# Six modulation weights summed on VectorE instead of multiplied on TensorE, and the first projection reordered

## What is computed

```python
mod_x = (jax.nn.silu(c) @ w_mod[i] + b_mod[i])[:, None, :]
mod_c = jax.nn.silu(c_ctx) @ w_mod[i] + b_mod[i]
sh1x, sc1x, g1x, sh2x, sc2x, g2x = jnp.split(mod_x, 6, axis=-1)
hx = modulate(rmsnorm(x, norm1_g[i]), sh1x, sc1x)
hc = modulate(rmsnorm(ctx, norm1_g[i]), sh1c, sc1c)
c_dq, c_dk, c_dv, c_gq, c_gk, c_gv = _mixer_heads(hc @ w_in[i])
x_dq, x_dk, x_dv, x_gq, x_gk, x_gv = _mixer_heads(hx @ w_in[i])
...
out_x = _mix_queries(...)          # differential + grouped attention, then w_out
x = x + g1x * out_x
hx2 = modulate(rmsnorm(x, norm2_g[i]), sh2x, sc2x)
x = x + g2x * peer(hx2, ...)       # 16 experts of 8 heads gathered per token
```

## Time and profile before

| | us |
|---|---|
| median of 3 runs | 1664.56 |
| lowest and highest run | 1661.77, 1664.97 |
| the profiled execution, its own time | 1663.03 |
| its span in the profile | 1661.2 |
| TensorE busy | 1407.2 |
| VectorE busy | 1086.2 |
| ScalarE busy | 617.1 |

### The profile page before, as it was taken

One profiled execution on the slowest core, in us unless ns is written; L12 is line 12 of the kernel. 1 busy time (PEld: TensorE's weight loads), 2 busy tenths in 40 slices (PEclk: granted clock), 3 DMA queues, 4 the chain that ended last, 5 costly groups with the idle time before them and its releaser, 6 DMA issues.

```text
span 1661.2 us, 20184 instructions
## 1 busy us (share of the span) xinstructions
PE 1407.2 (85%) x6400; PEld 968.6 (58%) x6400; DVE 1086.2 (65%) x2240; ACT 617.1 (37%) x1213; POOL 278.9 (17%) x263
## 2 busy tenths in 40 slices
PE   7897989578787878787877848978999889889998
PEld 2784666334343434343433317668999776689986
DVE  3667864666767676667677536647887366378863
ACT  4344642122222222222222114445665344456652
POOL 0000000444444444444444300000000000000000
PEclk9999989789898989899989978989999999899999
DMA  9423430799999999999999943133444431335440
GB/s 400 176 102 112 192 123 26 295 421 421 421 422 423 422 422 422 422 422 422 422 421 422 422 175 111 67 113 142 175 181 178 179 127 51 125 130 188 168 178 26
DMA packets 49267, 418.04 MB, mean 252 GB/s; under 512 B 5408, under 2 KB 5536, under 8 KB 6560
## 3 DMA queue, kind: packets, MB, share of 16 engines
q0 software_dynamic: 36864, 268.45, 38.9%
q1 hardware_dynamic: 12320, 148.51, 23.3%
HBM read 415.89 MB, written 1.05 MB: 251 GB/s over the span
## 4 chain that ended last, share of the span: by engine, by line
PE 57%; DMA 18%; DVE 8%; issue 8%; POOL 5%; ACT 3%; POOLq 0%; DVEq 0%; ACTq 0%; SPq 0%
DMA arena<-in_uv,ids 18%; PE ps L938 9%; PE ps L1134 5%; PE ps L1133 5%; PE ps L1135 5%; POOL arena L666 4%; PE ps L1009 4%; PE ps L1011 4%; PE ps L1010 4%; PE ps L918 2%; PE ps L1001 2%; PE ps L1059 2%; PE ps L788 2%; PE ps L790 2%; PE ps L789 2%
## 5 line engine op out<-in xcount | busy, mean ns | idle before, releaser
L938 PE MATMUL ps<-ring,arena 128*128 128x512 f32 x512 | 255.9, 662 | 105.4 <-ACT arena L1305 105.4
L536 DVE TENSOR_TENSOR arena_r<-ring,arena_r 128x1024 fp32r<-128x1024 f32 x168 | 204.7, 1224 | 89.2 <-ACT arena_r L530 89.1
L938 PE MATMUL ps<-arena 128*128 128x512 f32 x512 | 228.9, 606 | 31.3 <-ACT arena L1305 31.0
L938 PEld LDWEIGHTS ps<-ring,arena 128*128 128x128 f32 x512 | 107.8, 214 | 249.1 <-issue 133.0
L1739 DVE CUSTOM_DVE_ANT_0 arena<-arena 128x1024 f32<-128x1024 f32 x128 | 155.3, 1225 | 129.9 <-DMA arena<-in_uv,ids 129.7
L1305 ACT ACTIVATE arena<-cst,wts 128x128 f32<-128x128 f32 x256 | 89.5, 394 | 388.6 <-DVE wts L1731 272.5
L666 POOL DMA_INDIRECT ring<-in_uv,ids x128 | 134.8, 1053 | 549.0 <-issue 329.0
L530 ACT ACTIVATE arena_r<-ring 128x1024 fp32r<-128x1024 f32 x168 | 175.9, 1053 | 84.6 <-PE ps L1011 84.6
L1133 PE MATMUL ps<-hH,arena_r 128*128 128x256 f32 x704 | 199.4, 283 | 0.0
L1134 PE MATMUL ps<-arena_r 128*128 128x256 f32 x704 | 199.2, 283 | 0.0
L1135 PE MATMUL ps<-hH,arena_r 128*128 128x256 f32 x704 | 199.2, 283 | 0.0
(11 more groups left out here) (279 smaller groups left out, 2076.7 us busy)
## 6 DMA issues: line engine op xcount, KB each, us to landing
ring<-in_lw SPq DMA_DIRECT2D x42, 2048.0 KB, 8.4
ring<-in_b1w SPq DMA_DIRECT2D x18, 2048.0 KB, 7.7
wqb<-in_wq SPq DMA_DIRECT2D x8, 1024.0 KB
ring<-in_lw SPq DMA_DIRECT2D x6, 1024.0 KB, 5.0
ring<-in_uv,ids POOLq DMA_INDIRECT x128, 17.0
arena<-in_uv,ids POOLq DMA_INDIRECT x128, 18.7
cst<-in_const SPq DMA_DIRECT2D x1, 1736.0 KB, 20.0
skb<-in_ctx SPq DMA_DIRECT2D x1, 1024.0 KB, 14.2
```

The source lines that it names most:

```text
L536: nc.vector.tensor_tensor(wL[p % PIECES], piece_raw(p), wH[p % PIECES].bitcast(F32), ALU.subtract)\
L938: last = nc.tensor.matmul(ps[:, 4 + 2 * c + b, :], diag[:, k % 4, :], vrows[k][:, b * 512:(b + 1) * 512], start=False, stop=(close and k = ...
```

## The change

Each of the six `MOD_B` weights is no longer split and multiplied on TensorE. VectorE now forms, per partition, the sum over the eight k-tiles of weight times silu (`mod_part`: one `tensor_scalar` for the first tile, seven `scalar_tensor_tensor` after it, each 128x512, each waiting for the one before), and TensorE sums over the partitions with four small matmuls against a column of ones (`mod_total`). Only the x vector is summed. There are 48 such parts: 13 stand between the steps of the projection, eight before the copies of the turned keys and queries, two per unit in attention from unit 0 on (one in unit 13). The totals stand after piece 15 of the projection and after units 0, 3, 7, 11 and 15. The splitting pieces, the copies of the row sum and `mod_cols` for these weights go.

The projection now takes dk, kv, gq, dq, dv: queries fourth, values last. The six weights share the ring: the projection has slots 4, 5, 7, 9, 11 and the modulation weights 6, 8, 10, 12, 13, 14. The turning of keys and queries uses PSUM banks 4 to 7 instead of 0 to 3, and ScalarE copies the last values out ahead of its share of those tiles.

```diff
+IN_SLOT = (4, 5, 7, 9, 11)
+MODB_SLOT = (6, 8, 10, 12, 13, 14)
-IN_CHUNKS = ((0, 1, 2, 3), (0, 1, 2, 3), (2, 3), (0, 1, 2, 3), (2, 3))
-IN_BANK = (4, 0, 2, 0, 4)
+IN_CHUNKS = ((0, 1, 2, 3), (0, 1, 2, 3), (2, 3), (2, 3), (0, 1, 2, 3))
+IN_BANK = (4, 0, 2, 4, 0)
+TURN_BANK = 4
+MODB_UNIT = (0, 3, 7, 11, 15)
+MODB_EARLY = 21
...
+        def mod_part(dve, *parts):
+            for p in parts:
+                i, k = p // KD, p % KD
+                acc, weight = macc[:, i % 2, :], slot(MODB_SLOT[i])[:, k, :]
+                if k == 0:
+                    wait_slot(dve, MODB_SLOT[i])
+                    dve.wait_ge(modcol_done, max(MOD_A, MOD_A + i - 1))
+                    ins = nc.vector.tensor_scalar(acc, weight, sil2[:, k, 0:1], None, ALU.mult)
+                else:
+                    ins = nc.vector.scalar_tensor_tensor(acc, weight, sil2[:, k, 0:1], acc, ALU.mult, ALU.add)
+                ins.then_inc(mod_sum, 1)
+                dve.wait_ge(mod_sum, p + 1)
...
                 run(V.tensor_tensor(r3, r3, rstd[:, r0:r0 + nh].unsqueeze(2).broadcast_to([P, nh, HD]), ALU.mult))
+                if r0 == 0:
+                    piece(13)
                 run(V.tensor_tensor(r3, r3, con(gain).unsqueeze(1).broadcast_to([P, nh, HD]), ALU.mult))
                 if r0 == 0:
-                    piece(13)
+                    piece(14)
...
-                elif n < MOD_A + IN1:
-                    sp.wait_ge(in_lo, in_end(n - MOD_A))
-                elif n < OUT_AT:
-                    sp.wait_ge(m_lo, 4 * (n - MOD_A - IN1 + 1))
+                elif n in IN_SLOT:
+                    sp.wait_ge(in_lo, in_end(IN_SLOT.index(n)))
+                elif n in MODB_SLOT:
+                    sp.wait_ge(mod_sum, KD * (MODB_SLOT.index(n) + 1))
...
+            def mod_total(i, bank):
+                pe.wait_ge(mod_sum, KD * (i + 1))
+                for jj in range(4):
+                    last = nc.tensor.matmul(ps[:, bank, 2 * jj:2 * jj + 2], macc[:, i % 2, jj * P:(jj + 1) * P],
+                                            ones[:, 0:2], start=True, stop=True)
+                last.then_inc(modcol_done, 1)
...
+                if b == 4 and q == 1:
+                    pe.wait_ge(fills, 3)
+                    pe.wait_ge(proj_act, 8)
+                    mod_total(0, 4)
...
             for m in range(16):
-                i = MOD_A + m // 2
                 if m + 2 < 16:
                     scores(m + 2)
-                if m // 2 < MOD_B:
-                    if m % 2 == 0:
-                        pe.wait_ge(mod_out, i)
-                    mod_piece(2 * m, 7)
-                    mod_piece(2 * m + 1, 7)
                 turn(m)
                 if m >= 1:
                     values(m - 1)
-                if m % 2 == 1 and m // 2 < MOD_B:
-                    mod_cols(i, 7)
+                if m in MODB_UNIT:
+                    i = MODB_UNIT.index(m) + 1
+                    pe.wait_ge(mod_out, MOD_A + i)
+                    mod_total(i, 7)
             values(15)
...
-            in_rest(dve, 17)
-            dve.wait_ge(in_used, IP)
-            rotated(4, 2, 3)
-            rotated(4, 3, 4)
+            dve.wait_ge(in_used, in_end(3))
+            rotated(3, 2, 3)
+            rotated(3, 3, 4)
...
+            mod_bias(MOD_A, 4)
+            mod_part(dve, *range(13, MODB_EARLY))
+            leave(dve, ops_qk(), T_QK, 1, base=TURN_BANK)
...
                 if m + 2 < 16:
                     attn_max(m + 2)
-                mod_rest(dve, 2 * m + 2)
                 attn_out(m)
-                mod_rest(dve, 2 * m + 3)
+                mod_part(dve, *range(MODB_EARLY + 2 * m, min(MODB_EARLY + 2 * m + 2, KD * MOD_B)))
                 if m >= 1:
                     attn_rows(m - 1)
+                if m - 1 in MODB_UNIT:
+                    mod_bias(MOD_A + MODB_UNIT.index(m - 1) + 1, 7)
             attn_rows(15)
+            mod_bias(MOD_A + MOD_B - 1, 7)
```

More of the change, by code:

```diff
@@ L204, in program @@
         kT = area(8, 5, 512)
-        wHm = [area(kb, PIECE, of=arena_r) for kb in (48, 68, 76)]
-        wLm = [area(52, PIECE, of=arena_r), area(72, PIECE, of=arena_r), wqb_r[:, PIECE:2 * PIECE]]
+        macc = modrow
         E = area(18, 2, 2, 512)
@@ L363, in tile_free, with transposes @@
                 pe.wait_ge(tile_act if prev % 2 == 0 else tile_dve, off + prev // 2 + 1)
-        def transposes(pe, g0, tiles, off=0):
+        def transposes(pe, g0, tiles, off=0, base=0):
             for i, blocks in enumerate(tiles):
@@ L464, in in_raw @@
             b, q = IN_AT[p]
-            return ring[:, (MOD_A + b) % RING, q * PIECE:(q + 1) * PIECE]
+            return ring[:, IN_SLOT[b] % RING, q * PIECE:(q + 1) * PIECE]
         def in_high(act, *pieces):
@@ L702, in mod_rows @@
                 last.then_inc(mod_used, 1)
[L704 to L713, removed]
             def mod_cols(i, bank):
-                pe.wait_ge(modrow_out, i + 1)
+                pe.wait_ge(modrow_out, i + 1 if i < MOD_A else i + 1 - MOD_B)
                 for jj in range(4):
                     last = nc.tensor.matmul(ps[:, bank, 2 * jj:2 * jj + 2], mod_row(i)[:, jj * P:(jj + 1) * P],
-                                            con("sum4")[0:4, :] if mod_split(i) else ident[0:2, 0:2], start=True, stop=True)
+                                            con("sum4")[0:4, :] if i < MOD_A else ident[0:2, 0:2], start=True, stop=True)
+                last.then_inc(modcol_done, 1)
[4 more added lines that the diff above has]
+                                            ones[:, 0:2], start=True, stop=True)
                 last.then_inc(modcol_done, 1)
@@ L774, in _ @@
                 elif q == 0 and b == 3:
+                    pe.wait_ge(proj_dve, 2)
+                elif q == 0 and b == 4:
                     pe.wait_ge(proj_act, 6)
-                elif q == 0 and b == 4:
-                    pe.wait_ge(proj_dve, 2)
                 pe.wait_ge(in_lo, p + 1)
@@ L1232, in _ @@
             roots(24, 2)
-            in_high(act, 13, 14, 15, 16)
-            act.wait_ge(in_used, in_end(3))
-            for j in range(4):
-                rows_out(3, j)
-            in_high(act, 17)
+            in_high(act, 13, 14, 15, 16, 17)
             act.wait_ge(lam_sum, 1)
             nc.scalar.activation(lam[:, 0:2], lam[:, 2:4], ACT.Exp).then_inc(lam_exp, 1)
-            leave(act, ops_qk(), T_QK, 0)
+            act.wait_ge(in_used, IP)
+            for j in range(4):
+                rows_out(4, j)
+            leave(act, ops_qk(), T_QK, 0, base=TURN_BANK)
             act.wait_ge(tile_done, T_NORM2)
-            mod_high(act, 0, 1)
             gqa = 0
@@ L1254, in _ @@
                     act_pt(act, m - 1)
-                mod_high(act, 2 * m + 2, 2 * m + 3)
-                if m % 2 == 1 and m // 2 < MOD_B:
-                    mod_row_out(MOD_A + m // 2, 7)
             act_pt(act, 15)
@@ L2001 @@
     mods = [ktiles(wmod[:, i * 512:(i + 1) * 512]) for i in range(MODS)]
-    b1w = np.stack([slot_of(m) for m in mods[:MOD_A] + [ktiles(parts[n]) for n in ("dk", "kv", "gq", "dv", "dq")]
-                    + mods[MOD_A:MOD_A + MOD_B] + [ktiles(wout[:, i * 512:(i + 1) * 512]) for i in range(OUT1)]
-                    + mods[MOD_A + MOD_B:]])
+    early = {IN_SLOT[i]: ktiles(parts[n]) for i, n in enumerate(("dk", "kv", "gq", "dq", "dv"))}
+    early.update({MODB_SLOT[i]: mods[MOD_A + i] for i in range(MOD_B)})
+    b1w = np.stack([slot_of(m) for m in mods[:MOD_A] + [early[n] for n in range(MOD_A, OUT_AT)]
+                    + [ktiles(wout[:, i * 512:(i + 1) * 512]) for i in range(OUT1)] + mods[MOD_A + MOD_B:]])
     wq = np.stack([ktiles(a["peer_wq"][0][:, h * 256:(h + 1) * 256]) for h in range(PH)])
```

67 lines of the change are left out of this document (25 added, 42 removed).

## The result

The changed kernel takes **1653.7 us** (median of 4 runs, 1652.08 to 1654.99), the kernel before 1663.64 on the same chip (4 runs, 1661.77 to 1664.97). The ratio is 0.9939, with a 95% interval of 0.9925 to 0.9954: 9.9 us faster, where 13.9 were forecast. The profiled execution took 1652.99 with a span of 1651.2; against the 1661.2 before, that is 10.0.

What follows compares the result with a forecast made beforehand. It took the projection's matmuls, then VectorE's work in attention, as the bound. Terms -11.4 - 2.0 + 1.2 - 2.4 - 0.8 + 1.5 = -13.9 us against 1664.56 gave 1650.7, stated as 1650.6; own range 1647 to 1653, wider 1646 to 1658.

Steps and rivals of the forecast that it cites:

- Price of a part: One VectorE multiply-add of 128x512 in attention costs 0.79 us, two 1.58, read from the same operation at L1593.
- Start of attention: First scores to first reciprocal: without queued subtractions the reciprocal follows at 4.1 us instead of 6.1, -2.0 us.
- End of attention: Units 12 and 13, the last total and last bias: added parts and sums cost +1.2 us, up to +2.0.
- Projection: Reordered matmuls ahead of attention: pieces 12 and 13 late by 0.9 and 0.5 us, turning starts at 132.1, -2.4 us.
- The first rival: VectorE or a load is late ahead of turning: 2 to 4 us lost, about 1653.5 us; chance 0.10.
- The ring: Weight loads through shared slots: the values' load leaves at about 93.5, with some 10 us to land before piece 14.
- Attention, units 0 to 11: VectorE swaps two subtractions per unit for two multiply-adds: twelve units take 57.8 us against 69.24, -11.4 us.
- The clock: TensorE, with less work in differential units, runs partly at half clock: 0.4 us a unit, +1.5 us in all.
- The second rival: TensorE's clock swings, grouped units start at half clock: 1658 us at most, more likely 1656; chance 0.10.
- The third rival: TensorE stays at 1.2 GHz all through attention and becomes the bound: +29 us, so 1678; chance 0.04.
- The fourth: Gain given back after attention because the gathers are bound by something not starting earlier: 1664.6 us; chance 0.03.
- One sign named in advance: In attention, a last reciprocal of unit 12 later than 201 us would show the forecast wrong.

Runs made afterwards that it cites:

- fillers: Three idle matmuls added per differential unit (1 to 3, 8 to 11) between scores and turn, against the changed kernel: 1648.17 us, ratio 0.9908 to the kernel before.
- fillers and moved totals: Changed kernel plus three idle matmuls per differential unit, and totals behind units 0, 4, 7, 12, 14: 1646.41 us, ratio 0.9899 to the kernel before.

## Why the prediction was right, and where it was off

The sign held, and so did the mechanism: VectorE's work sets the pitch of the units, and the wait ahead of turning goes. The size was 4 us too large. 1653.7 lies 0.7 above the forecast's own range of 1647 to 1653 and inside the wider bounds of 1646 and 1658, which take in the rivals.

- **Price of a part**: taken as 0.79 from the same form of instruction; two take 1.53, 0.77 each. Differential units were put at 5.0 and take 5.0; grouped ones at 4.4 and take 4.2 to 4.5.
- **Start of attention**: -2.0 forecast, -1.9 measured.
- **End of attention**: +1.2 forecast, +1.8 measured, and the nearness is luck. 1.4 of it is the clock in unit 12. With fillers the same stretch takes 17.84 (197.43 to 215.27), only 0.35 over the 17.49 before, so the term by itself was too large. A total takes 0.95 at full clock. The row L874, from which I had 1.9 for eight passes, stood at half clock (0.50 from 234 to 240 us in the kernel before).
- **Projection**: pieces 12 and 13 were to be late by 0.9 and 0.5 and cost waits of 1.03 and 0.22. Turning was put at 132.1 and started at 131.85, the first scores at 137.8 and came at 137.85. Turning is split, with 0.90 of waiting for ScalarE inside, which first copies the values, as worked out. The last parts on VectorE did not run into it: they were done at 132.3, where I had put 134.1, and VectorE then waited 0.69 for its first tile. The first rival, something late ahead of turning, didn't come about.
- **The ring**: no wait for a load shows in the stretch.
- **Attention, units 0 to 11**: here the gain fell short, with a pitch of 5.05 us where 4.8 was named. Without the clock, -11.4 was too cautious by 1.1: with fillers the twelve units take 56.7, where 57.8 were forecast. With the clock they take 60.6.
- **The clock** is the mis-sized term. I took +1.5 for it: 0.4 in some differential units, because their matmuls nearly fit under VectorE even at 1.2 GHz. That part was right or too dear, as the differential units still take 5.0 at half clock (units 1 and 9 lose 0.3 each against the fillers). But I took the grouped units to be warm, since TensorE is busy 3.8 of 4.4 us in them, and overlooked that the first of them *starts* with whatever the differential units left. Against the 4.30 of both with fillers it cost 3.1 to 3.2 in unit 4 and 1.4 to 3.2 in unit 12, plus 0.9 at the output projection. Together it cost some 6 us in the profiled execution (3.9 in units 0 to 11, 1.4 in unit 12, up to 0.9 at the output projection), where +1.5 stood in the sum. That the total was off by only 4 is in part luck: the terms up to the end of attention were too cautious by 1.8 without the clock, and 1.1 was lost behind the first gather. The fillers, which change nothing else, bring back 4.4 us of the median.
- **The second rival** thus came true in part. It had the mechanism (grouped units meet half clock at their start) and its price (+3.2 each for two of them), and I gave it 0.10. Its total of 1656 to 1658 was too high, because the eight differential units lose 0.6 together, where it had 0.4 for each, and because the other terms were too cautious. (Its own sum, 6.4 + 3.2 - 1.5 on top of 1650.6, gives 1658.7.) The trace agrees with the rule that stood behind it, from the Trainium skill's page "TensorE: Matmul & The Clock Gate" (section "A second HAM failure mode: psum-queue depth-cycling"): the clock swung between its two levels, 0.50 to 1.00, while small idle spells of 0.9 to 2.4 us recurred.
- What misled me was one row: 2.77 of 5.00 us busy at a clock of 1.00. It lay just behind the projection, in which TensorE had been back to back. In the changed kernel that same place (142 to 148 us) also shows 1.00, and the stretches after it don't.
- **The third rival**, half clock throughout, didn't happen: in the grouped units the clock returns (0.77 from 166 to 172, then 1.00).
- **The fourth**, a gain given back in the gathers, didn't either. From the first gather to the end of the experts 690.2 us pass, against 689.4 in the kernel before.
- One sign named in advance failed: unit 12's reciprocal was to come by 201 and came at 202.66. The granted clock was to stay above 0.85 between 140 and 200 us, and it was 0.85 there (0.84 from 142 to 208).

What stays open: the fillers' gain is larger locally than in total. In its profiled execution the first gather starts at 281.90, 7.4 us before the 289.32 of the changed kernel run again, but the span is only 4.0 shorter. Of this, 2.6 us are lost in the two layers after the experts (674.4 instead of 671.8 us). The kernel with fillers and moved totals, whose layers are the same, needs 671.7 there, so it is no property of the fillers that these runs can show, and no run was made to find it. Nor is it settled why the clock of the same kernel stays low for some 3 us in unit 12 in one execution, which loses 1.4 us, and for 10 in another, which loses 3.2.

## What to carry to other kernels

When work is taken off TensorE on a path that another engine bounds, ask what its clock does in the idle time that is left, and price the loss not where TensorE idles but at the head of the next stretch in which it is needed: there everything between its last wait and the result that is waited for ran at half speed here. Two cheap cures were to put idle matmuls into the gaps, and to move TensorE work that nobody waits for (here a column sum) behind the work that is waited for. They cure one loss, so their gains don't add. And when an order is undone as an experiment, place the moved work as well as it was placed before, or the run measures the placement too (here about 2 of 5.3 us).

## What the runs showed of the hardware that was not expected

- Adding matmuls whose result nobody reads made a kernel 4.4 us faster, with the granted clock at 1.00 from 142 to 208 us instead of 0.84.
- A stretch in which TensorE was busy 3.61 of 6.00 us, with no idle time over 2.39 us (154 to 160), was followed by one at 0.50, while the earlier trace rows had 1.00 at 2.77 of 5.00. The busy time of a stretch alone didn't tell the clock. That what came before it counts too is my reading; no run varied it by itself.
- Once low, the clock stayed low for 10 us in which TensorE was busy without a gap (158.4 to 168.4 in the changed kernel's first trace, 198.4 to 208.4 in its second), and elsewhere for only 3 (199.4 to 202.6 in the first). Spells of 10 us cost 3.1 to 3.2 us in a unit, the short one 1.4.
- The column sum over 128 partitions (four products of 128x128 with two columns, in eight passes) took 0.95 us at 2.4 GHz and 1.71 at 1.2, no more than the 1.05 of the product with only four rows.
